# Moving two scratch transfers to another queue, the tables of turns to an earlier stage, and the matrix products to other blocks, in a one-core trunk of latent attention, gated MLP and S5

## What is computed

```
h = x
layer 0: h += latent_attention(rmsnorm(h)) @ w_o          # 8 heads, block-causal
         h += conv_ffn(rmsnorm(h))                         # d_ff 2816, three-tap causal conv, SiLU gate
layer 1: h += s5(rmsnorm(h));  h += conv_ffn(rmsnorm(h))
out = rmsnorm(h)

s5:  u = h @ w_in, 64 groups of 16 channels, 64 complex states each
     x[t] = a * x[t-1] + bbar u[t];  y = Re(c x) + d*u;  glu(gelu(y))
     a = exp(lam*dt), bbar = (a-1)/lam * b                 # depend on parameters only
```

## Time and profile before

| what | value |
|---|---|
| median of 3 runs | 1239.08 us (1238.88 to 1242.77) |
| profiled execution, own time | 1239.83 us |
| its span, first to last instruction | 1238.0 us |
| granted TensorE clock, mean | 0.960 |
| busy: PE, PEld, DVE, ACT, POOL | 1133.8, 919.4, 805.4, 455.5, 124.2 us |
| HBM | 125.6 MB, 101 GB/s |

### The profile page before, as it was taken

The page is one execution under the profiler, slowest core; times in us unless marked ns, Lnnn a source line. Parts: engine busy times, 40 slices in busy tenths (PEclk is TensorE's granted clock), DMA queues, the critical chain, the costliest instruction groups (busy, mean ns, idle before and its releaser), DMA issues.

```text
span 1238.0 us, 14622 instructions
## 1 busy us (share of the span) xinstructions
PE 1133.8 (92%) x5596; PEld 919.4 (74%) x5596; DVE 805.4 (65%) x1151; ACT 455.5 (37%) x677; POOL 124.2 (10%) x238
## 2 busy tenths in 40 slices
PE   6998999999509998999989998998999999999995
PEld 4776658887407887788867887787888888888874
DVE  6787555688218687887875885544776357744764
ACT  5413444444102254324535222433444234422441
POOL 3838000000560000000000000000000000000000
PEclk9999999999858998999999997998999999999997
DMA  6232002232103343343235685332232333233221
GB/s 208 82 98 69 1 1 85 86 102 86 34 34 120 103 136 102 102 137 119 94 94 170 198 251 140 113 100 85 86 102 85 104 101 103 85 102 102 87 84 68
DMA packets 61749, 125.60 MB, mean 101 GB/s; under 512 B 21744, under 2 KB 30320, under 8 KB 61680
## 3 DMA queue, kind: packets, MB, share of 16 engines
q1 hardware_dynamic: 58224, 112.09, 28.8%
q0 software_dynamic: 3456, 12.58, 2.8%
HBM read 109.97 MB, written 14.68 MB: 101 GB/s over the span
## 4 chain that ended last, share of the span: by engine, by line
PE 62%; issue 19%; DVE 6%; DMA 5%; POOLq 4%; POOL 2%; ACT 1%; SPq 1%; DVEq 1%; ACTq 0%
PE bank L1163 20%; PE bank L1164 20%; PE bank L1165 20%; DMA ud_scratch<-UB 2%; DMA yd_scratch<-Y 1%; DVE WL L642 1%; POOLq L1016 1%; POOLq L1021 1%; POOL s_t L1009 1%; POOLq L1019 1%; POOL PA L1009 1%; POOLq L1014 1%; PE bank L1329 1%; DVE SS L653 1%; PE bank L1181 1%
## 5 line engine op out<-in xcount | busy, mean ns | idle before, releaser
L409 ACT ACTIVATE WH<-RAW 128x1024 fp32r<-128x1024 f32 (+1 forms) x184 | 190.2, 1034 | 444.7 <-PE bank L1165 409.5
L1163 PE MATMUL bank<-GH,WH 128*128 128x512 f32 x816 | 325.1, 398 | 16.8 <-DVE GL L680 11.8
L1164 PE MATMUL bank<-GL,WH 128*128 128x512 f32 x816 | 320.8, 393 | 0.0
L1165 PE MATMUL bank<-GH,WL 128*128 128x512 f32 x816 | 320.5, 393 | 0.0
L1163 PE MATMUL bank<-AH,WH 128*128 128x512 f32 x596 | 237.2, 398 | 52.1 <-DVE AL L880 51.0
L642 DVE TENSOR_TENSOR WL<-RAW,WH 128x1024 fp32r<-128x1024 f32 (+1 forms) x184 | 221.6, 1205 | 48.5 <-ACT WH L409 48.1
L1164 PE MATMUL bank<-AL,WH 128*128 128x512 f32 x596 | 234.6, 394 | 0.0
L1165 PE MATMUL bank<-AH,WL 128*128 128x512 f32 x596 | 234.4, 393 | 0.0
L1163 PEld LDWEIGHTS bank<-GH,WH 128*128 128x128 f32 x816 | 155.1, 190 | 53.0 <-issue 17.8
L1164 PEld LDWEIGHTS bank<-GL,WH 128*128 128x128 f32 x816 | 155.1, 190 | 33.0 <-issue 1.2
L1165 PEld LDWEIGHTS bank<-GH,WL 128*128 128x128 f32 x816 | 155.0, 190 | 32.9
(11 more groups left out here) (230 smaller groups left out, 985.5 us busy)
## 6 DMA issues: line engine op xcount, KB each, us to landing
RAW<-in_w_up SPq DMA_DIRECT2D x88, 512.0 KB, 3.4
RAW<-in_w_dn SPq DMA_DIRECT2D x32, 512.0 KB, 3.4
RAW<-in_w_glu SPq DMA_DIRECT2D x16, 512.0 KB, 3.5
RAW<-in_w_dn SPq DMA_DIRECT2D x16, 384.0 KB, 3.0
RAW<-in_w_wo SPq DMA_DIRECT2D x8, 512.0 KB, 3.4
od_scratch<-OO POOLq DMA_DIRECT2D x8, 512.0 KB, 4.4
kd_scratch<-KT POOLq DMA_DIRECT2D x8, 512.0 KB, 4.3
RAW<-in_w_win SPq DMA_DIRECT2D x8, 512.0 KB, 4.7
```

What stands on the lines that cost most here:

```text
L409: act_(WH[b % RH][:, :n], RAW[b % RW][:, :n], ACT.Copy).then_inc(s_hi, 1)
L1163: mm(out, wh, hi_[:, k, :], start=start, stop=False)
L1164: mm(out, wh, lo_[:, k, :], start=False, stop=False)
L1165: return mm(out, wl, hi_[:, k, :], start=False, stop=stop)
```

## The change

Three things change. `spill(j)` and `lags(j)` are issued by SP, after the weight load whose number stands in `SPILL_AT`: the `OO` transfer after the load of block b+5 when operation 5 lies in block b, the `KT` transfer after the load of block n+6 when `matrices(j)` stands before block n. GpSimd starts the tables of turns when the eighth head's attention product is done (`s_pv`, `HEADS`), that is at the start of wo and not at the start of dn00. And a dn block now has four S5 operations instead of three, so that the 96 operations end with dn01; after an up block `matrices(j)` comes three blocks behind the last operation instead of two.

With the new counts, tile 1's operation 2 lies in block 38; tile 1's last operation in block 41 with `matrices(1)` before block 43; tile 2's in 44 with `matrices(2)` before 46; tile 3's in 47, before 50; tile 4's in 59, before 62; tile 5's in 65, before 67; tile 6's in 68, before 70; tile 7's in 71, before 74.

```diff
 for _b in FFN0:
-    _n = 1 if PHASE_OF[_b].startswith("up") else 3
-    OPS_AT[_b] = range(_i, min(_i + _n, MAT_OPS * NJ))
+    _up = PHASE_OF[_b].startswith("up")
+    OPS_AT[_b] = range(_i, min(_i + (1 if _up else 4), MAT_OPS * NJ))
     _i = OPS_AT[_b].stop
-            _n = _b + 2
+    for _o in OPS_AT[_b]:
+        if _o % MAT_OPS == MAT_OPS // 2 - 1:
+            SPILL_AT[_b + 5] = ("O", _o // MAT_OPS)
+        if _o % MAT_OPS == MAT_OPS - 1:
+            _n = _b + (3 if _up else 2)
             while _n - FIRST[PHASE_OF[_n]] < 2:
                 _n += 1
+            MAT_AT[_n] = _o // MAT_OPS
+            SPILL_AT[_n + 6] = ("K", _o // MAT_OPS)
...
+            def spill(j):
+                sp.wait_ge(s_O, j + 1)
+                sp.dma_start(OD[j], OO[:].rearrange("p r q c s -> p r (q c s)")).then_inc(s_ow, 16)
+            def lags(j):
+                sp.wait_ge(s_kt, j + 1)
+                sp.dma_start(KD_[j], KT[:]).then_inc(s_kw, 16)
             for b in range(4, FIRST["win"] + 4):
                 load(b)
+                if b in SPILL_AT:
+                    what, j = SPILL_AT[b]
+                    if what == "O":
+                        spill(j)
+                    else:
+                        lags(j)
...
-            pool.wait_ge(s_mm, FIRST["dn00"])
+            pool.wait_ge(s_pv, HEADS)
...
-            def spill(j):
-                pool.wait_ge(s_O, j + 1)
-                g.dma_start(OD[j], OO[:].rearrange("p r q c s -> p r (q c s)")).then_inc(s_ow, 16)
-            def lags(j):
-                pool.wait_ge(s_kt, j + 1)
-                g.dma_start(KD_[j], KT[:]).then_inc(s_kw, 16)
-            for j in range(NJ):
-                spill(j)
-                lags(j)
```

More of the change, by code:

```diff
@@ L123 @@
 OPS_AT = {}
+MAT_AT = {}
+SPILL_AT = {}
 _i = 0
 for _b in FFN0:
-    _n = 1 if PHASE_OF[_b].startswith("up") else 3
-    OPS_AT[_b] = range(_i, min(_i + _n, MAT_OPS * NJ))
+    _up = PHASE_OF[_b].startswith("up")
+    OPS_AT[_b] = range(_i, min(_i + (1 if _up else 4), MAT_OPS * NJ))
     _i = OPS_AT[_b].stop
[L129 to L133, removed]
-            _n = _b + 2
+    for _o in OPS_AT[_b]:
[3 more added lines that the diff above has]
+            _n = _b + (3 if _up else 2)
             while _n - FIRST[PHASE_OF[_n]] < 2:
                 _n += 1
-            MAT_AT[_n] = _i // MAT_OPS
-assert len(MAT_AT) == NJ and max(MAT_AT) + 1 < FIRST["win"]
+            MAT_AT[_n] = _o // MAT_OPS
+            SPILL_AT[_n + 6] = ("K", _o // MAT_OPS)
+assert _i == MAT_OPS * NJ and len(MAT_AT) == NJ and len(SPILL_AT) == 2 * NJ
 def build(nc, d):
```

## The result

The changed kernel takes 1191.72 us (median of 4 runs, 1189.92 to 1195.40) against 1238.98 us (4 runs, 1234.57 to 1242.77) for the one before: a ratio of 0.9611, with a 95% interval of 0.9583 to 0.9639. The forecast was 1194 us, in a range of 1185 to 1204. The profiled execution took 1195.40 us, and its span is 1193.3 us. Lines have moved by 15 or so (in helper matmuls by 3): WL is L657, X L811, OO L845 and L852, GM L868, AL L895, and the transposes that open `matrices(j)` L1324. The products on `ET` are L1332.

A forecast was written before the change was run, and what follows sets the result against it. TensorE sets the pace in layer 0's MLP, stopped when VectorE is late. From 1239.8 us, 62.5 go and 9.6, 3.5 and 4.3 come: 1194.7, or 1194 against the median; range 1185 to 1204.

The forecast's parts named there:

- (1): Layer 0's MLP: the wait for tile 0's OO transfer goes, giving TensorE back 47.5 us.
- (4): Before dn02: TensorE's wait for AL and the slow matmuls after it go, 0.8 us of wait and 1.7 of clock.
- (3): Before the transposes that open matrices(j): waits of 7.5 us go, and a low clock of about 1.8 us.
- Four operations in a dn block: dn00 and dn01: VectorE falls behind, so TensorE waits before matrices(1), (2), (5) and (6), 9.6 us added.
- The clock: After three new waits, two in dn stages and one before dn00, the clock falls: 0 to 5.4 us, taken as 3.5.
- The tables beside VectorE: wo and up00: GpSimd's tables and VectorE's SBUF operations exclude each other, 4.3 us added, bounds 0 and 20.
- The 1.6 us for GM: TensorE's 1.6 us wait for GM goes but returns as a wait for AL before dn00.
- SP's queue: Transfers and waits among SP's weight loads: no load waits longer, with 4.6 us of cover, so 0 counted.
- A: Rival: hardly any new wait, 3 to 8 us come, 1180 to 1185, or 1185 to 1189 with one; chance 0.17.
- B: Rival: the tables weigh more, VectorE losing every contest; 25 to 35 us come, 1201 to 1212; chance 0.17.
- C: Rival: SP's 16 transfers each hold a weight load by 4.4 us, 70 us come, 1247, slower than before; chance 0.02.
- D: Rival: the stall moves to a later transfer awaited in dn00, under 3 us a case; shares the forecast's chance, 0.64.

The follow-up runs named there:

- e4: The changed kernel with matrices(j) three blocks behind its last operation after a dn block too, instead of two: 1175.06 us, ratio 0.9482.
- e9: The kernel of e4 run again on another chip, beside the changed kernel: 1178.31 us, ratio 0.9494.
- e11: The changed kernel itself run again, on the same chip as e9: 1191.80 us, ratio 0.9607.
- e6: The changed kernel without the tables of turns, two memsets in their place: 1192.12 us, ratio 0.9627.
- e1: The changed kernel with GpSimd's tables started at dn00 again, the transfers staying with SP: 1199.20 us, ratio 0.9674.
- e3: The changed kernel with three S5 operations in a dn block and matrices two blocks behind everywhere, as before: 1194.66 us, ratio 0.9637.
- e2: The changed kernel with both scratch transfers issued by GpSimd again, behind the early tables: 1190.98 us, ratio 0.9603.
- e7: The changed kernel with the tables of turns made twice, the second pass lying in up00: 1206.09 us, ratio 0.9738.

## Why the prediction was right

*What goes.* Forecast 62.5 us. The wait for tile 0's transfer is gone with its 47.5 us; AL stands at 1.8 for three stages (50.2 before), as term (1) and (4) say together. The waits of 7.5 and 1.6 us are gone too, as (3) says, and the low clock of 372.60 to 378.00 with them: 336 to 343 has a new one of its own. The term of 0.8 at win's start can't be told from the rest.

*Four operations in a dn block.* Forecast 3.4 to 3.6 before matrices(1) and (5) and 1.2 before (2) and (6), 9.6 in all; measured 3.77, 3.82, 1.41 and 1.43, together 10.4, and none before (3) and (7). The count of 11.6 us of VectorE's work against 8.2 of TensorE's came out at 11.7 against 8.1. This is shown twice over, by the trace and by e4, which moves the place and nothing else.

*The clock.* Forecast 3.5 for three waits of such a size; there were two, since the third, before dn00, did not come. The two stretches show 0.52 and 0.63, and e9 against e11 leaves 3.1 us for them and the rest.

*The tables beside VectorE*: this is the term that was mis-sized. Forecast 4.3 us, 3.4 of them lateness carried into up00 and 0.9 for SS; measured 0.6 for SS and nothing else, and by e6 nothing that a run can tell. The step that failed is "that leaves GpSimd 3.0 a block", which took VectorE's WL, GL and SS, 2.4 us a block, as locking GpSimd out for their full length, and with it the "about 5 us" that were to be left for up00. From 207.85 to 225.43 GpSimd did operations worth 11.6 us alone in 17.6 us, which is 3.6 in a block of 5.44. The tables ended at 238.14 and not near 245, at the first Z of up00 (238.2; before 237.5). Three differences add up to the 5 us: of the 38.07 us 1.3 were the two transfers' issues behind the tables, which alone are 36.67; by 225.4 some 26.6 of these were done and not 24; and the last nine operations, 10.1 us alone, fitted in by 238.14 where some 9 were counted.

The reading of the earlier trace rows was not at fault. An engine that starts just behind the other's operation does lose nearly a whole one: GpSimd's WC lost 1.07 us behind WL, VectorE's SS 1.10 at 229.35 behind an operation of GpSimd begun at 229.02. That is the exclusive lock, held for the whole instruction, of the Trainium skill ("SBUF — State Buffer", section "SBUF: two separate sides"). But where both engines have a queue of such work, a turn of both takes 1.7 us and not the 2.15 of two whole operations (e1), so by the measurement the price of a meeting is less than a whole operation: GpSimd's 36.67 us became 49.39, 12.7 more, where the forecast held it up for 8 x 2.4 = 19.2 us in the eight blocks of wo. Why a turn is shorter than the two operations was not settled.

*The 1.6 us for GM* that I let return as a wait for AL before dn00: it did not return. The wait there was 0.5 us, where I forecast 3 to 5. In e3, where GM's wait of 1.6 comes back, AL's wait before dn00 is 0.4: VectorE's place at the end of up00 does not hang on it.

*SP's queue.* Forecast 0, and e2 shows it: the same waits with the transfers on either queue. SP waited 13.2 us for OO, eight times, at most 1.9. One load of w_dn was late for ScalarE's WH, by 1.5 us, and TensorE has no wait from it. That wait is not there before or in e2, so it belongs to SP's queue.

*The sum.* Of measured terms, what went up to win is 48.4 (AL) + 7.5 + 1.6, and by the prediction's own count 5.9 of clock: 63.4. New are 10.4 and 0.6 of waits. RSTD of win came 47.5 us earlier, so 63.4 - 11.0 - 47.5 = 4.9 us came besides, a remainder, of which about 3 is the clock behind the two waits (e9 against e11). The rest is no more than executions of this kernel differ by: from 330 to 350 and from 470 to 500 its clock stood at 0.83 and 0.89, in e11 at 0.91 and 0.94, and there RSTD came 2.5 us earlier still, at 629.66. With the S5 stage's 2.8 the span fell by 44.7; forecast was 62.5 - 17.4 = 45.1. That they agree within 0.4 us is luck: the tables were 3.7 too dear and GM's 1.6 did not return, against 0.8 more of waits before the transposes, 0.8 at win's start that did not show, 1.4 in the remainder beyond my 3.5 of clock, and the 2.8 of the S5 stage, which is chance. By the medians the result lies 2.3 us below the forecast.

*The rivals.* A (hardly any new wait) was right on the tables and wrong on the dn blocks, so the result does not lie the 5 to 14 us below the forecast that it would have brought. B fell. e7 shows that its mechanism exists, with the tables in up00 and not in wo: 1206 us. C fell with this result and with e2; its own sum was wrong too, as 1247 leaves out the 17.4 us that the forecast adds in any case. With them it is 1194.7 + 70 = 1265, and it would decide from 2.8 us a transfer on and not from 3.9. D did not occur: no OO waits for a later transfer.

## What to carry to other kernels

A long stretch of computation in front of a transfer on the same in-order queue holds whatever waits for that transfer: look for the transfer's issue time, and take either of them out, since one is enough. Where a consumer on the bounding engine stands a fixed number of blocks behind its producer, try one block more before making the producer faster; the limit is the next write into the same buffer, and spreading the producer's work can move that limit. Before putting work beside an engine that is seen to slow it down, look at that engine's idle time in the stage: the same tables cost nothing that can be told beside 28 us of idle time in 57, and 12 to 15 us where VectorE had 5 idle in 52.

## What the hardware showed that I had not expected

GpSimd and VectorE, both with operands in SBUF, take turns, and both pay: in 56.6 us GpSimd's work grew from 36.67 to 49.39 us and VectorE's from 28.91 to 38.67. When VectorE was busier, beside dn00 and up01 in e1, the same tables grew to 62.13 us. X, which takes one of its inputs from a bank, kept its 0.68 to 0.69 us throughout wo. And behind both waits of 3.8 us the granted clock was at its lower level (matmul steps of 0.43 us against 0.23). Behind the wait of 1.41 at 358.26 it was not: the matmuls from 361.69 on step by 0.23 in the chain.
